# The ends of a mixture-of-experts stage: first block by a product, last two experts kept on chip

## The reference, cut to what matters

```
logits = x2d @ w_router + router_bias
scores = softmax(logits)                       # 16 experts in 4 groups; the best group, the best 2 in it
weights = top_vals / sum(top_vals)
# every expert gets the rows of its tokens in blocks of EXPERT_BLOCK rows
h = silu(xblk @ w_gate[e]) * (xblk @ w_up[e])  # 1024 -> 512
y = (h @ w_down[e]) * gate                     # 512 -> 1024
f = segment_sum(y, token)                      # both rows of a token added
x = layer_norm(DEEPNORM_ALPHA * x + f, ln2_g, ln2_b)
```

## Time and profile before

| | us |
|---|---|
| median of the timed runs | 3306.8 |
| the profiled execution | 3296.8 |
| its span | 3295.1 |
| TensorE matmuls busy in the span | 3001.5 (91%) |
| VectorE busy | 1879.5 (57%) |
| ScalarE busy | 1142.3 (35%) |
| GpSimd busy | 329.7 (10%) |

### The profile page before, as it was taken

The page is one execution under the profiler, slowest core; times in us unless marked ns, Lnnn a source line. Parts: engine busy times, 40 slices in busy tenths (PEclk is TensorE's granted clock), DMA queues, the critical chain, the costliest instruction groups (busy, mean ns, idle before and its releaser), DMA issues. The chain is left out here.

```text
span 3295.1 us, 35668 instructions
## 1 busy us (share of the span) xinstructions
PE 3001.5 (91%) x13808; PEld 2388.0 (72%) x13808; DVE 1879.5 (57%) x2809; ACT 1142.3 (35%) x1969; POOL 329.7 (10%) x480
## 2 busy tenths in 40 slices
PE   7979999889999899999998799979999999879994
PEld 6768877777776776777776688767677777657883
...
GB/s 123 71 58 93 99 21 78 79 92 106 294 1 72 83 90 80 77 14 86 91 92 178 253 403 404 276 122 103 68 89 4 87 90 90 187 223 352 405 410 142
DMA packets 154831, 468.21 MB, mean 142 GB/s; under 512 B 16014, under 2 KB 33320, under 8 KB 129320
## 3 DMA queue, kind: packets, MB, share of 16 engines
...
## 5 line engine op out<-in xcount | busy, mean ns | idle before, releaser
L167 DVE CAST weights_r<-weights 128x1024 fp32r<-128x1024 f32 (+4 forms) x248 | 206.2, 831 | 719.4 <-DMA weights<-in_w_in 289.8
L154 PE MATMUL ps<-x_cols_hi_r,weights_r 128*128 128x512 f32 x896 | 360.0, 402 | 2.8 <-DVE weights_r L352 1.4
L169 DVE TENSOR_TENSOR weights_r<-weights,weights_r 128x1024 fp32r<-128x1024 f32 (+4 forms) x248 | 353.6, 1426 | 8.5
L156 PE MATMUL ps<-x_cols_hi_r,weights_r 128*128 128x512 f32 x896 | 356.1, 397 | 0.0
L155 PE MATMUL ps<-x_cols_lo_r,weights_r 128*128 128x512 f32 x896 | 356.0, 397 | 0.0
L1055 POOL TENSOR_SCALAR weights<-weights,weight 128x256 f32<-128x256 f32 (+3 forms) x304 | 151.7, 518 | 671.6 <-DVE weight L949 408.4
L999 ACT ACTIVATE weights<-weights,minus_top 128x256 f32<-128x256 f32 (+3 forms) x304 | 166.8, 550 | 117.6 <-DVE minus_top L912 117.5
L154 PEld LDWEIGHTS ps<-x_cols_hi_r,weights_r 128*128 128x128 f32 x896 | 169.8, 190 | 48.6 <-issue 4.6
L155 PEld LDWEIGHTS ps<-x_cols_lo_r,weights_r 128*128 128x128 f32 x896 | 169.7, 189 | 41.7 <-issue 1.4
L156 PEld LDWEIGHTS ps<-x_cols_hi_r,weights_r 128*128 128x128 f32 x896 | 169.3, 189 | 41.2
L162 PE MATMUL ps<-ident 128*128 128x128 f32 x734 | 109.0, 308 | 80.5 <-PEq L89 32.3
...
## 6 DMA issues: line engine op xcount, KB each, us to landing
...
block_x<-expert_x_rows SPq DMA_DIRECT2D x33, 512.0 KB, 8.7
expert_y_rows<-block_y POOLq DMA_DIRECT2D x33, 512.0 KB, 8.1
...
```

The lines of the kernel that those rows point to most:

```text
L154: pe.matmul(out, as_r(left[1]), as_r(right[0]), start=start, stop=False)
L156: return pe.matmul(out, as_r(left[0]), as_r(right[0]), start=False, stop=stop)
L167: dve.tensor_copy(as_r(hi), lo).then_inc(rounded, 1)
L169: dve.tensor_tensor(as_r(lo), lo, as_r(hi).bitcast(F32), ALU.subtract).then_inc(done, 1)
```

## The change

Five things are changed in the two expert stages and the stages that follow them.

1. In `route`, ScalarE rounds the first four weight pieces between its copies of columns, and VectorE splits them ahead of the choice of experts.
2. VectorE makes a table with a 1 where a token is row n of expert 0's first block, and TensorE gets block 0's columns directly as products of x with that table; its rows are no longer loaded from DRAM. Twelve idle products stand ahead of the rank products, the 26 later ones are gone. Later blocks' rows still come from DRAM; SyncE waits for the scatter ahead of the loop.
3. In the loop ScalarE rounds the next block's gate pieces ahead of taking the output, and the up pieces behind it.
4. Outputs of experts 14 and 15 stay on chip (`kept.rows`, in the place of the first gate piece's high part). VectorE makes tables of their places and shares by token, TensorE turns them beside the last expert. GpSimd gathers the other rows when the store of expert 13 has landed and the ring's rooms are free; VectorE joins them to x, two token tiles at the end of its list for expert 14, two behind its list for expert 15.
5. The combining stage spreads the kept rows by four f32 products per token tile with the turned table, adds them to x from PSUM, and normalises as before.

```diff
+        pe.wait_ge(s.rows_chosen, 1)
+        for half in range(2):
+            for k in range(4):
+                for t in range(TT):
+                    mm = pe.matmul(m.ps[:, half * BANK + k * P:half * BANK + (k + 1) * P], x[:, t, 4 * half + k:D:DK], first_rows[:, t, :],
+                                   start=k == 0 and t == 0, stop=k == 3 and t == TT - 1)
+            mm.then_inc(s.first_x_turned, 1)
...
         for k in range(DK):
             act.wait_ge(s.col_turned, k + 1)
             act.activation(xT[:, k, :], m.ps[:, (k % 6) * BANK:(k % 6 + 1) * BANK], ACT.Copy).then_inc(s.col_taken, 1)
+            if k == 0:
+                act.wait_ge(m.expert_fetched, fetched)
+            if k < 4:
+                round_piece(act, hi[k], raw[k], s.first_rounded)
...
         link(dve.memset(earlier[:, :, :], 0.0))
         for e in range(4):
             link(dve.memset(order[:, e:e + 1], 4.0 - e))
+        for p in GATE + UP:
+            dve.wait_ge(s.first_rounded, p + 1)
+            split_piece(dve, hi[p], raw[p], s.first_split)
...
         tt(place[:, :, :], by_tile(rank_bank), earlier[:, :, :], ALU.add)
+        link(dve.scalar_tensor_tensor(out=own_place[:, :], in0=place[:, :, 0], scalar=1.0, in1=picked[:, :, 0], op0=ALU.add, op1=ALU.mult))
+        dve.tensor_tensor(first_rows, c.number[:, 1:1 + P].unsqueeze(1).broadcast_to([P, TT, P]), own_place[:, :].unsqueeze(2).broadcast_to([P, TT, P]),
+                          ALU.is_equal).then_inc(s.rows_chosen, 1)
+        link(dve.scalar_tensor_tensor(out=tail.place[:, :, :], in0=place[:, :, KEPT:], scalar=1.0, in1=picked[:, :, KEPT:], op0=ALU.add, op1=ALU.mult))
+        tt(tail.share[:, :, :], pick[:, 0, :, KEPT:], spread(moe.share[:, :, 0], N_EXPERTS - KEPT), ALU.mult)
+        tt(tail.other[:, :, :], pick[:, 1, :, KEPT:], spread(moe.share[:, :, 1], N_EXPERTS - KEPT), ALU.mult)
+        tt(tail.share[:, :, :], tail.share[:, :, :], tail.other[:, :, :], ALU.add)
...
+KEPT = N_EXPERTS - 2
...
+        free = [room[KEPT, p] for p in UP + DOWN]
+        gathered = [flat(raw[r])[:, i * D:(i + 1) * D] for r in free for i in range(2)]
+        tail = bag(**{n: sb(f"tail_{n}", [P, TT, N_EXPERTS - KEPT]) for n in ("place", "share", "other")},
+                   by_token=ye[:, :].rearrange("p (n t) -> p n t", n=N_EXPERTS - KEPT))
+        route(block, s, sb, m, router, columns, x, moe, hi, raw, 16 * RAW_ROOMS * (layer + 1), xe[:, 0:TT * P].rearrange("p (t n) -> p t n", t=TT), tail)
...
             sp.sem_inc(s.first_y_left, 1)
-            sp.wait_ge(s.copied, 16 * 2 * TT)
-            sp.dma_start(xe[:, :], rows_at(moe.x_rows, 0)).then_inc(s.first_x_loaded, 16)
...
             sp.wait_ge(s.tabled, 5)
+            sp.wait_ge(s.copied, 16 * 2 * TT)
             with sp.Fori(0, late) as i:
...
-            pe.wait_ge(s.tabled, 5)
-            idle_products(pe, m, 20)
-            pe.wait_ge(s.copied, 16 * 2 * TT)
-            idle_products(pe, m, 6)
-            pe.wait_ge(s.first_x_loaded, 16)
-            turn_x(s.first_x_turned)
             with pe.Fori(0, late) as i:
                 pe.wait_ge(s.first_x_split, 2 * i + 2)
                 for p in GATE + UP:
                     pe.wait_ge(s.first_split, 6 * i + (p + 1))
                     project(xT[0], p, p, gate_bank if p in GATE else up_bank, s.first_used)
-                pe.wait_ge(s.first_x_loaded, 16 * i + 32)
+                pe.wait_ge(s.first_x_loaded, 16 * i + 16)
                 turn_x(s.first_x_turned)
...
+                if b == LAST:
+                    pe.wait_ge(s.tail_made, TT * (N_EXPERTS - KEPT))
+                    for n, at_bank in enumerate((7, x_bank)):
+                        for t in range(TT):
+                            mm = pe.transpose(m.ps[:, at_bank * BANK + t * P:at_bank * BANK + (t + 1) * P], tail.by_token[:, n, t * P:(t + 1) * P],
+                                              m.ident[:, :])
+                        mm.then_inc(s.tail_turned, 1)
                 pe.wait_ge(s.hidden_done, b)
...
                 round_x(xT[0], s.first_x_turned, 2 * i + 2, s.first_x_rounded)
-                act.wait_ge(s.first_used, 6 * i + 12)
-                act.wait_ge(s.first_y_left, i + 1)
-                take_out(s.first_out_taken)
                 for p in GATE + UP:
+                    if p == UP[0]:
+                        act.wait_ge(s.first_used, 6 * i + 12)
+                        act.wait_ge(s.first_y_left, i + 1)
+                        take_out(s.first_out_taken)
                     act.wait_ge(s.first_loaded[p], 16 * i + 32)
                     act.wait_ge(s.first_used, 6 * i + (7 + p))
-                    round_piece(p, p, s.first_rounded)
+                    round_piece(act, hi[p], raw[p], s.first_rounded)
...
             def static_take_out(b):
                 act.wait_ge(s.used, at[b, 5] + 1)
+                if b >= KEPT:
+                    return take_out(s.out_taken, kept.rows[b - KEPT])
                 if b > 1:
...
                 round_pieces(b, DOWN)
                 if b < LAST:
                     round_pieces(b + 1, UP[:1])
+                else:
+                    for n, at_bank in enumerate((7, x_bank)):
+                        act.wait_ge(s.tail_turned, n + 1)
+                        act.activation(kept.by_row[:, n, :], bank(at_bank), ACT.Copy).then_inc(s.tail_taken, 1)
                 act.wait_ge(s.h_turned, b)
...
+            def join(t):
+                for i in range(2):
+                    dve.wait_ge(s.gathered[2 * t + i], 16)
+                    if i:
+                        dve.wait_ge(s.joined, 2 * t + 1)
+                    else:
+                        dve.wait_ge(s.x_scaled, TT)
+                    dve.scalar_tensor_tensor(out=x[:, t, :], in0=gathered[2 * t + i], scalar=moe.share[:, t, i:i + 1], in1=x[:, t, :],
+                                             op0=ALU.mult, op1=ALU.add).then_inc(s.joined, 1)
...
-                split_pieces(b, DOWN)
+                split_pieces(b, DOWN if b < LAST else DOWN[:1])
                 dve.wait_ge(s.silu_done, b)
                 dve.wait_ge(s.used, at[b, 3] + 1)
                 if b > 1:
                     dve.wait_ge(s.h_turned, b - 1)
                 hidden(s.hidden_done)
+                if b == LAST:
+                    split_pieces(b, DOWN[1:])
                 if b < LAST:
                     split_pieces(b + 1, UP[:1])
                 dve.wait_ge(s.h_rounded, b)
@@ -2766,6 +2810,17 @@
...
+                elif b < LAST:
+                    dve.wait_ge(s.y_stored, 16 * (KEPT - 1))
+                    for n in range(N_EXPERTS - KEPT):
+                        for t in range(TT):
+                            dve.tensor_scalar(tail.by_token[:, n, t * P:(t + 1) * P], router.number[:, 1:1 + P], tail.place[:, t, n:n + 1],
+                                              tail.share[:, t, n:n + 1], ALU.is_equal, ALU.mult).then_inc(s.tail_made, 1)
+                    join(0)
+                    join(1)
+                else:
+                    join(2)
+                    join(3)
...
-            for b in range(1, N_EXPERTS):
+                pool.tensor_scalar(x[:, t, :], x[:, t, :], ALPHA, 1.0, ALU.mult, ALU.mult).then_inc(s.x_scaled, 1)
+            for b in range(1, KEPT):
                 pool.wait_ge(s.out_taken, 2 * b)
                 pool.dma_start(rows_at(moe.y_rows, MAX_OVER + b), ye[:, :]).then_inc(s.y_stored, 16)
-            pool.wait_ge(s.y_stored, 16 * LAST)
+            pool.wait_ge(s.y_stored, 16 * (KEPT - 1))
+            for t in range(TT):
+                if t == 0:
+                    pool.wait_ge(s.used, at[KEPT, UP[1]] + 1)
+                if t == 2:
+                    pool.wait_ge(s.used, at[KEPT, DOWN[1]] + 1)
+                for i in range(2):
+                    n = i * TT + t
+                    pool.indirect_dma_start(out=gathered[2 * t + i], out_offset=None, in_=moe.y_rows,
+                                            in_offset=bass.IndirectOffsetOnAxis(ap=moe.slot[:, n:n + 1], axis=0)).then_inc(s.gathered[2 * t + i], 16)
...
+            def spread(t):
+                for n, row in enumerate(kept.rows):
+                    for half in range(2):
+                        mm = pe.matmul(m.ps[:, (2 * t + half) * BANK:(2 * t + half + 1) * BANK], kept.by_row[:, n, t * P:(t + 1) * P],
+                                       row[:, half * 512:(half + 1) * 512], start=n == 0, stop=n == len(kept.rows) - 1)
+                mm.then_inc(s.spread, 1)
+
+            def shifts(t):
+                pe.wait_ge(s.added, 2 * t + 2)
+                idle_products(pe, m, 4, 2 * t)
+                for k in range(DK):
+                    pe.matmul(region(DK * t + k), t_.b[:, k * P:(k + 1) * P], m.ident[:, :], start=k % 4 == 0, stop=False)
+
...
+            spread(0)
+            spread(1)
+            if xT:
                 pe.wait_ge(s.rows_loaded, 32)
                 shifts(0)
-                for t in range(TT):
```

(25 more changed lines are left out.)

103 lines of the change are left out of this document (38 added, 65 removed).

## The result

The changed kernel takes 3264.3 us in the median of four runs (3257.07 to 3271.02), the kernel before 3305.5 beside it (3303.94 to 3309.93): ratio 0.9873, 95% interval 0.9849 to 0.9896. It is faster by 41 us, or 1.3%. The time lies inside the range of 3224 to 3269, but 20 us above the 3244 predicted and outside the forecast's own range of 3232 to 3256, to which it gave 62%. The profiled execution took 3265.1 (span 3263.4), 31.7 less than the one of before; that one lay 9 us under its median, this one at it, so the profiles show only 31.7 of the 41.

A forecast was written before the change was run, and what follows sets the result against it. TensorE bounds the regular stretch; gains lie at its ends: fronts -17 and -21.7, last experts 2 x -2.0, stage changes 2 x -4.6, combining -7.1 and -4.1; sum -63.1, 3244 us. Own range 3232 to 3256 (62%), outer 3224 to 3269.

The forecast's parts named there:

- The back: End of each expert stage: last output's store and change of stage, -4.6 us per layer (bounds -3.2, -5.6).
- Combining: Combining stage: gathers, weighting and first join go; -7.1 us in layer 1, -4.1 in layer 0.
- The front's logits: Routing: early roundings on ScalarE make the logits end 5.5 us later (bounds +2 and +8.5).
- The columns' products: Front: 32 f32 products of x with the table take 7.1 us, or 9 to 14 at 1.2 GHz.
- the down products behind them: Front of layer 0: 24 down products at 0.234 us take 5.6 instead of 6.93, as gaps ahead are shorter.
- the front of layer 0: Start of layer 0's expert part, from routing through the early blocks: -17 us (bounds -10, -21).
- The scatter: Front: eight issues at 0.95 us, ending 13 us after the start instead of 17.7 (bounds 12 and 17.7).
- The wait of 3.07: TensorE's 3.07 us wait for a split between blocks goes, once in layer 0 and twice in layer 1.
- The last expert: Last expert of each layer: TensorE's wait for hidden shrinks, -2.0 us per layer (bounds -1.0, -2.7).
- The regular stretch and the stage ahead: Middle experts, with TensorE busy 18.00 of 18 us, and the stage before routing: predicted change 0.
- (a): Rival at the fronts: loads take the front's gain back, -37 us in all, 3270; chance 10%.
- (d): Rival: roundings delay logits and the slow scatter's end sets all, fronts -4 and -9, 3269; chance 9%.

The follow-up runs named there:

- the second profile: The changed kernel run again without an edit, beside the kernel before: 3264.6 us, ratio 0.9878.
- the second version: Against the changed kernel: x copied into column order, old address spacing, more idle products, roundings behind alternate copies, some joins moved later: 3235.5 us, ratio 0.9781.

## Why the prediction was right or wrong, step by step

The number lies in the range, and the sum came out near for the end of the stage. At the front two terms were mis-sized, and the forecast's own range was missed for it.

The back: **right**. Store and change of stage 5.3 a layer against 4.6 (inside 3.2 to 5.6); 1.19 us are left of the 6.54, where 1.9 was taken. The forecast left one piece out that the trace of before holds, a DRAIN on GpSimd between the landing of the store and the barrier:

```profile
L85 POOLq DRAIN  x1: 2113/2113/2113, 3254.6 to 3254.6; - x1
```

The 6.54 of layer 1 are 0.3 to the store's issue, 2.9 to its landing, 0.2, this 2.1 (2.0 in layer 0) and 1.1 for the meeting of the engines. In the changed kernel GpSimd issues nothing behind the gathers and its drain is over 5 to 8 us before the barrier. So the estimate of 3.5 by the Trainium skill (DMA: Bandwidth & Descriptors, Anatomy of one DMA) was too small for what it left to the change of stage, not for the transfer: 3.2 were put on that, and the trace has 2.9. Why the drain takes 2 us is open.

Combining -7.2 against -7.1 in layer 1, with the first centring 7.0 us into the stage as forecast. In layer 0 it is -4.1 against -4.1, but there the working gave 35 to 38 of 39 us, that is -1 to -4, and the forecast took the favourable end without a reason: that it fits to the tenth is partly luck.

The front's logits: **right, with the size near**. +4.1 and +3.5 against +5.5 (bounds 2 and 8.5). The loads were to land 2.5 us into the stage ("about 1785", the stage starts at 1782.6). In this profile the first rounding begins 2.38 into the stage, and 1.84 in layer 1:

```profile
1789.84 1.91 ACT L2214 ACTIVATE weights_r<-x_cols_hi 128x2048 fp32r<-128x2048 f32 x1 [1.11 <-DMA weights<-in_w_exp_up]
```

The last copy of columns ends 13.9 into the stage against 13.4. What the forecast did not see is how much the landing varies: the same kernel had 3.81 in the second profile, with logits at 18.6, and the one with the copied x 6.42, with logits at 20.4 and so 8.5 lost.

The columns' products: **the step that failed**. "Ten such products, idle ones, are the row x20 ... 32 are 7.1 us, or 9 to 14": the idle ones read a matrix whose values lie side by side, these read every eighth value of x. They took 15.5, more than the upper bound for half clock. That put the first product and the down products of layer 0 at -5.9 instead of -11.9, and in layer 1 the down products at -6.5. In the run with the copied x the products are 5.9 us shorter in each layer. The second step that failed is the down products behind them, counted as 24 at 0.234 = 5.6 us, since "the gaps ahead are shorter": in layer 0 they took 8.5 (6.9 before), as 14 of them ran at 1.2 GHz, 0.43 us apart. Together the two are 8.9 us, about what the front of layer 0 lacks (-8.5 against -17). In the second version, with columns' products of 7.4 and first down products at full clock in layer 0, the fronts are 19.9 and 19.0 us shorter than before the change, 38.9 in sum against 38.7 predicted; that version has the other mends as well.

The scatter: **right**. Issues of 0.95, the second block's load issued 45.4 us into the stage against 46.1 (1828.7) predicted. Two differences nearly cancel in it: the scatter began 29.6 into the stage instead of 31.6, and the load followed 15.8 after that instead of 14.5. In this kernel it was not what set the end: TensorE turns the rows without a wait.

The wait of 3.07: **right**; gone at all three places, worth 7.3 us in the median and 9.7 in the profiles.

The last expert: **wrong**. The price of lateness was named ("each us by which gathers are later is one us on hidden"), the size was not: the first two gathers took 3.04 and 3.00 us to issue beside VectorE's splits, not the 0.95 that lies behind "every 1.25 us". So the rows of the second and third came late, and VectorE waited 0.89 and 1.00 us for them. -2.0 became +0.8 and +1.5. Whether the first gather is long differs from run to run: in other runs it took 1.03, and the stretch between the two last turns of hidden was 1.1 to 1.6 us shorter.

```profile
2113.95 3.04 POOL L2847 DMA_INDIRECT x_cols_hi<-expert_y_rows,slot  x1 [7.14 <-DMA expert_y_rows<-block_y]
2117.30 3.00 POOL L2847 DMA_INDIRECT x_cols_hi<-expert_y_rows,slot  x1 [0.30 <-issue]
2120.60 0.94 POOL L2847 DMA_INDIRECT x_cols_hi<-expert_y_rows,slot  x1 [0.30 <-issue]
```

The third was issued beside the tables, which have one input in on-chip memory, and took 0.94.

The regular stretch and the stage ahead, which the sum left out: **wrong by 7 us** (2.2 and 4.8). The addresses explain 2.2 + 2 x 0.9 = 4.0. The rest goes with the half clock at the end of the stage ahead, which differs from profile to profile; its cause was not tried.

The rivals: (a), loads that take the gain back, did not decide in this kernel, since the first block was late itself; waits for rows stand in the second version (2.2 to 2.7 us). (d), the scatter sets all, gave nearly the measured time (3269) for another reason, and (a) did so with 3270: the time alone could not have told the three apart. What stays open is which address bits slow the products, why one DMA engine ended late in one run, and how much of the stage ahead's spread (58.3 to 61.0) is chance.
